# Low part of the T4 weight sum on GpSimd, in four quarters, in place of VectorE

## The reference, cut to what matters

```
ffn = jnp.square(jax.nn.relu(h @ w1[l])) @ w2[l]
h = layer_norm(DN_ALPHA * h + ffn, ln2_g[l], ln2_b[l])
```

## Time and profile before

| | |
|---|---|
| Median of three runs | 1079.35 us (1078.64 to 1080.85) |
| The profiled execution's own time | 1078.98 us |
| Its span, first to last instruction | 1077.2 us |
| Around the span | 1.8 us |
| TensorE busy | 1056.3 us, 98% |
| VectorE busy | 794.8 us, 74% |
| ScalarE busy | 506.5 us, 47% |
| GpSimd busy | 91.2 us, 8% |

### The profile page before, as it was taken

The page is one execution under the profiler, slowest core; times in us unless marked ns, Lnnn a source line. Parts: engine busy times, 40 slices in busy tenths (PEclk is TensorE's granted clock), DMA queues, the critical chain, the costliest instruction groups (busy, mean ns, idle before and its releaser), DMA issues.

```text
span 1077.2 us, 15569 instructions
## 1 busy us (share of the span) xinstructions
PE 1056.3 (98%) x5310; PEld 896.5 (83%) x5310; DVE 794.8 (74%) x1108; ACT 506.5 (47%) x754; POOL 91.2 (8%) x84
## 2 busy tenths in 40 slices
PE   7999999999999999999999999999999999999996
PEld 6888889998888888888778888899888888888884
DVE  7855886968757757758977568777794784784788
ACT  3432666365355355355323347653743643643650
POOL 5200222100000000000002003221000000000001
PEclk9999999999999999999999999999999999999999
DMA  8422013030521521421333410310334134134122
GB/s 286 157 108 87 2 60 119 1 124 25 211 79 40 183 90 39 169 105 61 113 109 152 156 40 20 116 43 12 115 116 158 40 117 157 39 103 170 40 78 79
DMA packets 17380, 105.52 MB, mean 98 GB/s; under 512 B 2016, under 2 KB 2704, under 8 KB 5792
## 3 DMA queue, kind: packets, MB, share of 16 engines
q1 hardware_dynamic: 15984, 98.70, 25.2%
q0 software_dynamic: 1184, 5.86, 1.7%
q10 hardware_dynamic: 144, 0.07, 0.0%
HBM read 101.49 MB, written 2.10 MB: 96 GB/s over the span
## 4 chain that ended last, share of the span: by engine, by line
PE 92%; DVE 5%; issue 2%; ACT 0%; DMA 0%; DVEq 0%
PE bank L446 18%; PE bank L448 18%; PE bank L447 18%; PE bank L750 8%; PE bank L752 8%; PE bank L751 8%; PE bank L696 4%; PE bank L682 2%; PE bank L593 1%; PE bank L455 1%; PE bank L594 1%; DVE x L1539 1%; DVE w_lo L1142 1%; PE bank L527 1%; PE bank L606 1%
## 5 line engine op out<-in xcount | busy, mean ns | idle before, releaser
L446 PE MATMUL bank<-h_hi,w_hi 128*128 128x512 f32 (+1 forms) x704 | 260.8, 370 | 0.3
L447 PE MATMUL bank<-h_lo,w_hi 128*128 128x512 f32 (+1 forms) x704 | 260.3, 370 | 0.0
L448 PE MATMUL bank<-h_hi,w_lo 128*128 128x512 f32 (+1 forms) x704 | 260.3, 370 | 0.0
L750 PE MATMUL bank<-w_hi,hid_hi 128*128 128x512 f32 x448 | 174.6, 390 | 1.6 <-DVE x L1539 1.6
L751 PE MATMUL bank<-w_lo,hid_hi 128*128 128x512 f32 x448 | 174.3, 389 | 0.0
L752 PE MATMUL bank<-w_hi,hid_lo 128*128 128x512 f32 x448 | 174.3, 389 | 0.0
L1142 DVE TENSOR_TENSOR w_lo<-w_raw,w_hi 128x2048 fp32r<-128x2048 f32 x62 | 141.8, 2288 | 36.8 <-ACT w_hi L867 30.0
L446 PEld LDWEIGHTS bank<-h_hi,w_hi 128*128 128x128 f32 x704 | 132.6, 188 | 23.4 <-issue 1.1
L447 PEld LDWEIGHTS bank<-h_lo,w_hi 128*128 128x128 f32 x704 | 132.7, 188 | 22.4
L448 PEld LDWEIGHTS bank<-h_hi,w_lo 128*128 128x128 f32 x704 | 132.6, 188 | 22.4
L867 ACT CAST w_hi<-w_raw 128x2048 fp32r<-128x2048 f32 x56 | 107.1, 1913 | 78.9 <-PE bank L752 56.4
(11 more groups left out here) (167 smaller groups left out, 1634.0 us busy)
## 6 DMA issues: line engine op xcount, KB each, us to landing
w_raw<-in_weights SPq DMA_DIRECT2D x63, 1024.0 KB, 4.8
w_third<-in_weights SPq DMA_DIRECT2D x23, 1024.0 KB, 4.8
rows<-in_rows POOLq DMA_DIRECT2D x4, 1024.0 KB, 5.0
w_raw<-in_weights SPq DMA_DIRECT2D x4, 512.0 KB, 7.6
out_h<-x SPq DMA_DIRECT2D x8, 256.0 KB, 2.0
x<-in_x SPq DMA_DIRECT2D x3, 512.0 KB, 9.9
dft<-in_dft SPq DMA_DIRECT2D x2, 512.0 KB, 6.8
qk_gain<-in_qk_gain POOLq DMA_DIRECT2D x3, 192.0 KB, 3.3
```

The source lines that it names most:

```text
L446: pe.matmul(dst, s_hi, m_hi, start=first, stop=False)
L447: pe.matmul(dst, s_hi, m_lo, start=False, stop=False)
L448: return pe.matmul(dst, s_lo, m_hi, start=False, stop=last)
L750: pe.matmul(bank[dst + t][:], s_hi, m_hi, start=start, stop=False, skip_group_check=goes_on)
```

## The change

VectorE no longer makes the low part of T4. GpSimd makes it, in four instructions of 512 columns each, of which the last counts `w_lo`. It does so for each of the four chunks of a layer, after its loads for the next layer's mixers and before the load of `rows` (in `after` the lines from 1582 on stand one to two lines lower, those behind the new loop ten lines lower). Since `w_lo` is counted by two engines now, VectorE waits, before its next low part, until T4's is counted.

```
@@ -1571,13 +1571,14 @@
                     low(B21)
                     add(4)
                     add(5)
-                    low(T4)
                     add(6)
                     add(7)
                     add(8)
                     if not last:
                         add(9)
                         add(10)
+
+                        dve.wait_ge(sems["w_lo"], operand(l, c, T4 + 1))
                         low(CHUNK_OPERANDS + W0)
...
@@ -1708,6 +1710,14 @@
                         split_low(l, 13)
                 layer_norm_rstd(2 * l + 1, TOK - 1)
                 load_params(l + 1)
+                for c in range(CHUNKS):
+
+                    wait(pool, l, "w_hi", operand(0, c, T4 + 1))
+                    wait(pool, l, "w_lo", operand(0, c, T4))
+                    for part in range(PARTS):
+                        q = slice(part * PART, (part + 1) * PART)
+                        done = pool.tensor_tensor(w_lo[:, SLOT[T4], q], w_raw[:, 0, q], w_hi[:, SLOT[T4], q].bitcast(F32), ALU.subtract)
+                    done.then_inc(sems["w_lo"], 1)
 
                 wait(pool, l, "hidden_lo", 12 * CHUNKS)
                 load_rows(2 * l + 2)
```

## The result

| | before | after |
|---|---|---|
| Median | 1078.77 us (6 runs, 1078.36 to 1080.85) | 1083.58 us (6 runs, 1083.19 to 1084.11) |
| Ratio, 95% interval | | 1.0043 [1.0033, 1.0053] |
| Profiled execution, own time | 1078.98 | 1083.53 |
| Its span | 1077.2 | 1081.8 |

The change makes the kernel slower, by 4.6 us by the ratio and by the two profiled executions (the medians differ by 4.8). 1084.1 us was forecast, with 1081.2 to 1086.8 as the range.

The account below looks back on a forecast made before the run. TensorE was taken to bound the kernel, with VectorE counting only at the two layer closes. Gain 0 and cost 2.53 + 2.54 = 5.1 us on 1078.98 gave 1084.1 us, range 1081.2 to 1086.8.

Parts of the forecast that it names:

- What bounds: Whole kernel: TensorE, busy 98%, waits for VectorE only where a layer closes, 2.1 us together; the six other chunks cost 0.
- Quarters: GpSimd's T4 low part in each chunk: four quarters take 5.01 us, starting 0.09 us after B21's low part ends.
- The gap to the load and its landing: Layer closes: 0.16 us from quarters to the `rows` DMA, 5.0 to landing, 0.1 to `centre`, 2.5 us later.
- The 0.9 us that `add(8)` gains: Layer 0's close: `add(8)` starts at 524.5, not 525.42, so `centre` could start 0.9 us earlier.
- rival 1: Layer closes: the load of `rows` arrives in time, each layer gains 0.9 us, 1077.2 us in all; 4%.
- Interference: GpSimd's quarters beside VectorE's adds and statistics, one SBUF input each: counted as 0.
- The clock: Layer ends: TensorE idles 3.1 us and the granted clock might halve, taking the time above 1088.0 us; 1%.
- Rival 3: Layer ends: granted clock falls to half while TensorE idles 3.1 us, time above 1088.0 us; 1%.
- The sum: Whole kernel: gain 0, cost 2.53 + 2.54 = 5.1 us on 1078.98, giving 1084.1 us.
- late gains: Layer closes: `centre` waits for the `rows` load queued behind T4's quarters, 2.53 and 2.54 us later.

Follow-up runs that it names:

- e2: The changed kernel with the closing chunk's T4 low part left on VectorE, GpSimd making it only in the other three chunks: 1078.91 us, 0.9996 of the kernel before.
- e1: The changed kernel with the load of `rows` issued ahead of the last chunk's T4 quarters in each layer: 1077.34 us, 0.9985 of the kernel before.
- e3: The kernel before, with the load of `rows` also waiting for the last chunk's T4 low part, no work moved: 1081.86 us, ratio 1.0030.
- e5: The changed kernel with T4's low part in one GpSimd instruction of 2048 columns instead of four quarters: 1082.84 us, 1.0037 of the kernel before.
- e6: The changed kernel with 24 identity transposes ahead of TensorE's wait for `add(10)` in the closing chunk: 1083.33 us, 1.0038 of the kernel before.
- e4: The kernel before, with the load of `rows` also waiting for the last chunk's `add(8)`, no work moved: 1088.34 us, ratio 1.0088.

## Why the prediction was right

- **What bounds**: right. The two closes are where TensorE waits for VectorE, and e2 shows that the rest is neutral.
- **Quarters**: 5.04 us against 5.01 forecast, each 1.28 to 1.30 us.
- **The gap to the load and its landing**: 0.16 forecast and none found; `centre` started 5.15 and 5.01 us after the load's start, against 5.1. Measured from B21, `centre` is 529.12 - 527.27 + 0.54 = 2.4 us late in layer 0 and 4.19 - 1.94 = 2.25 in layer 1; 2.5 was forecast for each. The gap was the mis-sized term: the load starts at 523.97, and the last quarter ends at 518.99 + 5.04 = 524.03.
- **The 0.9 us that `add(8)` gains**: right, and e1 turns it into 1.6 us for the two layers, where rival 1 had 1.8. The time was worked out as 1077.2 there and is 1077.34.
- **Interference**: rightly counted at nothing. GpSimd's quarters ran beside VectorE's adds without either being stretched: the quarters took 1.28 to 1.30 us each, and the adds beside them 0.67 to 0.69, as before. In the changed profile GpSimd's `rstd` took 1.0 us beside a `centre` (two SBUF inputs) and 0.55 or 0.56 where VectorE was idle or went into an add (one SBUF input). The Trainium skill's rule on the shared read port ("SBUF — State Buffer", "Who interferes with whom"), that a VectorE instruction with two SBUF inputs contends with a GpSimd instruction that reads SBUF and one with at most one, outside its two-port modes, does not, agrees with this.
- **The clock**: wrong. Rival 3 was given 1% because the clock was still granted at 1.00 while TensorE had nothing to do from 1067 to 1072. The next five microseconds of the kernel before show what that row left out (windows, the same columns):

```profile
1072.00:1077.00 5.00, 0.00 (x0) 0.00 (x0) 2.72 (x5) 0.00 (x0) 1.01 (x1) 0.51 0.28 105
```

  The clock does fall after idle time, only later; a single place where it had not yet fallen was no evidence. What was also wrong is its price: above 1088 was named, and the fall cost 0.25 to 0.37 us in all, since most of it went into waits that were there anyway.
- **The sum**: 5.1 forecast for the two closes, 5.1 found. It is made up differently: 2.4 + 2.25 of late gains where 2.53 + 2.54 stood, the rest from the clock in layer 1 and about 0.1 in layer 0 that no run explains. That the two sums agree this closely is luck: the late gains were forecast 0.4 us too high, and the clock, left out, gives about as much back. The 4.6 between the two profiled executions is less by what the opening of the second was shorter.

## What to carry to other kernels

When work is moved to an engine that looks idle, look for what is queued behind it there, the DMAs above all: a load that was issued 16 us too early costs nothing until it stands behind work that ends too late. Put such a load ahead of the work that is moved; here the place of one load decided between 4.6 us lost and 1.6 us won. Work taken from an engine pays only where another engine waits for it: six of eight moved blocks were worth nothing, and the two others 0.8 us each (1.6 us in two layers, with the load put first).

## What the runs showed of the hardware

- After TensorE had nothing to do, the granted clock fell to the lower level after times that differ: about 2.4 us after the idle began in layer 0 of the changed kernel, in the midst of a wait; about 4.1 us after it in layer 1, when TensorE was at work again; and only after 5 us at the end of the kernel before. In e3, with idle times of 2.1 and 1.8 us, it stayed at 1.00; in e5, with 2.4 and 2.6, it fell in both layers. With filler transposes during the wait (e6) it stayed at 1.00 at both closes. At the closes it stayed low for 3.4 us each time in the changed kernel, and for 6.8 us in e4, where TensorE idled 5 us. The windows of e3 that hold its two waits (the same columns as above):

```profile
532.00:540.00 8.00, 4.92 (x26) 3.90 (x26) 7.52 (x14) 3.25 (x6) 0.55 (x1) 1.00 0.26 79
1060.00:1072.00 12.00, 7.61 (x33) 5.61 (x31) 11.31 (x21) 0.00 (x0) 1.56 (x2) 1.00 0.24 89
```

- While it was low, back-to-back 128x512 matmuls started 0.43 us apart in place of 0.23, and eight transposes took 1.97 us in place of 1.09.
- Splitting a subtraction of 2048 columns in four on GpSimd cost 0.4 us (5.04 against 4.63 in e5).
